# Low-key score products of a windowed attention layer in halves of TensorE's rows, on Trainium2

## The chip, the core and the metric
The kernel runs on one NeuronCore of a Trainium2 chip. The metric is the time on the device in microseconds for one execution of the whole program. The engines are TensorE (PE in the profile; its weight loads have a row of their own, PEld), VectorE (DVE), ScalarE (ACT), GpSimd (POOL) and SyncE (SP), which issues most DMAs.

## The reference, cut to what matters
Two groups of 512 tokens pass through the same two layers: layer A (latent attention) and layer B (windowed attention with 16 query heads, 2 key heads and 64 channels a head). The change lies in layer B, in this part:

```python
def swa_mixer(q, k, v, q_norm, k_norm, sink):
    q = rmsnorm(q.reshape(B, S, SWA_HEADS, SWA_HEAD_DIM), q_norm)
    k = rmsnorm(k.reshape(B, S, SWA_KV_HEADS, SWA_HEAD_DIM), k_norm)
    ...
    rel = jnp.arange(3 * BLOCK)[None, :] - BLOCK - jnp.arange(BLOCK)[:, None]
    in_window = jnp.abs(rel) <= WINDOW
    ...
        s = jnp.einsum('bqkgd,bjkd->bkgqj', q_blk, k_blk).astype(jnp.float32) * scale
        s = jnp.where(valid, s - slopes * dist, NEG)
        ...
        p = jax.nn.softmax(jnp.concatenate([s, sk], axis=-1), axis=-1)[..., :-1]
        return jnp.einsum('bkgqj,bjkd->bqkgd', p.astype(v_blk.dtype), v_blk)
```

With blocks of 128 tokens, query block i of the four meets the key blocks i-1 to i+1 that exist: 256 keys for blocks 0 and 3, 384 for blocks 1 and 2.

## The kernel before
The program runs four layers in turn, L = 0 to 3: A and B of the first group of tokens, A and B of the second. Every product keeps nearly full fp32 precision by splitting operands into a high part, rounded to fp32r, and a low part, the rest. A product of split operands is three matmuls: high by high, high by low, low by high (`mm3`).

In layer B the 64 channels of a head fill only half of TensorE's 128 rows, so the queries are stacked. `b_q(j)` handles head pair j: TensorE transposes the pair's queries into one bank (`b_q` of the TensorE part, line 2365), 64 rows for each head. ACT copies each half times its gain to `qT[half(a), j % 3, a, :]` as the high part (function `hi`, its activations have the line L859), and DVE writes the low part into the other half of the rows (function `lo`, L1283). `b_k(c)` puts the keys into `krT[:, 0, 0, :]` (high) and `krT[:, 0, 1, :]` (low), each twice, in both halves of the rows. One matmul over 128 rows then gives (high + low query) by high key, a second one by low key: `mm2`, lines 2063 and 2064. The low by low part, which the second one adds, is not needed.

`b_s(h)` makes the scores of head h: two matmuls for each of the four query blocks, in three banks: block 1, block 2, and blocks 0 and 3 together (`SHARED`, `SHARED_AT`). Each bank is told full after its last product. On DVE `b_max` (L1789) adds the bias and finds the maximum, and so frees the banks; ACT's `b_exp` (L886) and GpSimd's `b_p` (L1928) make the probabilities; `b_pt` (TensorE transposes L2102, ACT copies L859, DVE L1281, all to `probT`) turns them; `b_o` (L2415) multiplies them by the values; `b_low` (ACT, L1210, to `o_low`) and `b_sum` (DVE, L1803, to `o_pair`) add up high and low columns of the output.

The order on TensorE is written out by hand. Before the loop: projections, `b_q(0)`, `b_k(0)`, projections, `b_s(0)`, `b_q(1)`, ... In the loop over h = 0 to 15: `b_s(h + 2)`, projection steps (`fill`), `b_q(h // 2 + 2)` for even h up to 10, `b_o(h)`, projection steps, `b_pt(h + 1)`. ACT's and DVE's queues follow the same order: on ACT for an even h the copies of `b_q`, then `b_low(h)`, the tanh of gates that are complete (L896), the exps of head h + 2 and the copies of `b_pt(h + 1)`; on DVE `b_max(h + 2)`, the low halves of `b_q`, the gates (L1375), `b_sum(h)` and the low halves of `b_pt(h + 1)`.

Banks are handed on by counting semaphores: `vacant(use)` waits until the bank's use before has been read, `full(use)` tells that TensorE is through, `read(use)` that its reader is. A planner at the head of the file gives out banks; the scores of head 9 get for their first bank the one that `b_o(6)` wrote and `b_sum(6)` reads. `hi_done` counts ACT's high copies; a `lo` on DVE waits until as many are done as stood before it, plus `ahead`.

Of the kernel before, what the change touches and what calls it, by code (L numbers as in the profile page):

```python
# [11 lines left out]
P = 128  # L12
# [400 lines left out]
def span(i):  # L413

    return (window(i)[1] - window(i)[0] + 1) * P
# [6 lines left out]
def trunk_kernel(nc, kept, x, mem, mem_cols, w_a, w_b, w_out, w_mem, w_qb, w_kvb, gains, rope_gq, rope_gk, sink, cos, sin,  # L422
# [3 lines left out]
    with ctx:  # L426
# [4 lines left out]
        def place(name, shape, dt, at=None):  # L431

            size = int(np.prod(shape[1:])) * 4
            off = top[0] if at is None else at
            if at is None:
                top[0] += (size + 31) // 32 * 32
            return nc.alloc_sbuf_tensor_at(name, shape, dt, offset=off), off
# [25 lines left out]
        q_st, o_q = place("q_st", [P, NT, 2 * QK], fp32)  # L463
        k_st, o_k = place("k_st", [P, NT, 2 * QK], fp32)
        probT2, _ = place("probT2", [P, 2, 2 * 3 * P + CH], fp32r, o_q)
        c_st, _ = place("c_st", [P, NT, QR + KVR], fp32, o_q)
        k_mem_st, _ = place("k_mem_st", [P, NM, MW], fp32, o_k)
        sq, _ = place("sq", [P, 2, CH], fp32)
# [46 lines left out]
        with ExitStack() as turn, ExitStack() as block_end:  # L515
# [69 lines left out]
            def bank(use):  # L585
                return psum[USES[use][0]]
# [14 lines left out]
            def read(use):  # L601

                return bank_read[USES[use][0]], USES[use][1]
# [14 lines left out]
            def vacant(use):  # L618

                return bank_read[USES[use][0]], USES[use][1] - 1  # L620
# [56 lines left out]
            def half(a):  # L677

                return slice(64 * a, 64 * a + 64)
# [154 lines left out]
            def _(act):  # L834
# [20 lines left out]
                def hi(use, out, in_, gain=None, first=True):  # L855

                    if first:
                        act.wait_ge(*full(use))
                    act.activation(out, in_, ACT.Copy, scale=1.0 if gain is None else gain).then_inc(hi_done, 1)  # L859
# [126 lines left out]
                for L in range(LAYERS):  # L986
# [179 lines left out]
                    else:  # L1166
# [12 lines left out]

                        def b_q(j):  # L1180
                            for a in range(2):
                                hi(("bqT", L, j), qT[half(a), j % 3, a, :], bank(("bqT", L, j))[half(a), :],
                                   gcol[half(a), GAIN_AT["bq"]:GAIN_AT["bq"] + 1], first=a == 0)

                        def b_k(c):
                            hi(("bkT", L, c), krT[:, 0, 0, :], bank(("bkT", L, c))[:], gcol[:, GAIN_AT["bk"]:GAIN_AT["bk"] + 1])
# [66 lines left out]
            def _(dve):  # L1253
# [251 lines left out]
                for L in range(LAYERS):  # L1505
# [235 lines left out]
                    else:  # L1741
# [20 lines left out]
                        def b_q(j):  # L1762
                            for a in range(2):
                                lo(("bqT", L, j), qT[half(1 - a), j % 3, a, :], bank(("bqT", L, j))[half(a), :],
                                   qT[half(a), j % 3, a, :], gcol[half(a), GAIN_AT["bq"]:GAIN_AT["bq"] + 1], last=a == 1)

                        def b_k(c):
                            lo(("bkT", L, c), krT[:, 0, 1, :], bank(("bkT", L, c))[:], krT[:, 0, 0, :],
# [283 lines left out]
            def _(pe):  # L2052
# [8 lines left out]
                def mm2(out, lhs, rhs, start):  # L2061

                    nc.tensor.matmul(out, lhs, rhs[0], start=start, stop=False)  # L2063
                    return nc.tensor.matmul(out, lhs, rhs[1], start=False, stop=True)  # L2064
# [78 lines left out]
                for L in range(LAYERS):  # L2143
# [217 lines left out]
                    else:  # L2361
# [18 lines left out]
                        def b_s(h):  # L2380
                            pe.wait_ge(*read(("bqT", L, h // 2)))
                            pe.wait_ge(*read(("bkT", L, h // (HB // KVB))))
                            for s, blocks in enumerate(SHARED):
                                use = ("bS", L, h, s)
                                pe.wait_ge(*vacant(use))
                                for i in blocks:
                                    c = SHARED_AT[i][1]
                                    ins = mm2(bank(use)[:, c:c + span(i)], qT[:, (h // 2) % 3, h % 2, i * P:(i + 1) * P],
                                              tuple(krT[:, 0, a, window(i)[0] * P:(window(i)[1] + 1) * P] for a in range(2)), True)
                                ins.then_inc(full(use)[0], 1)  # L2390

                        def b_pt(h):
                            for s, blocks in enumerate(SHARED):
# [106 lines left out]
```

## Time and profile before

| | us |
|---|---|
| median of the runs | 1351.1 |
| lowest and highest of 3 runs | 1350.52, 1354.14 |
| the profiled execution | 1349.92 |
| its span in the profile | 1348.1 |

| engine | busy us | share of the span |
|---|---|---|
| PE | 1339.7 | 99% |
| PEld | 1163.8 | 86% |
| DVE | 890.7 | 66% |
| ACT | 678.0 | 50% |
| POOL | 395.3 | 29% |

The first layer B's attention lies at about 515 to 648 us, the second's at 1183 to 1315. Times in rows are counted from the span's start. Matmuls are pipelined: the duration of one reaches from its start to its modelled end, and the next one starts while it is still under way, so the pace of TensorE is read from starts. Consecutive equal instructions stand in one row of a timeline, with their count behind the x and the time from the first one's start to the last one's end. A bracket at the end of a row gives the engine's idle time before it and the instruction that ended it.

### The profile page before, as it was taken

Reading aid. Unit: us, or ns where it says so; the run is one execution under the profiler, and the core shown is the slowest. Engines: PE = TensorE matmul, PEld = TensorE weight load, DVE = VectorE, ACT = ScalarE, POOL = GpSimd, SP = SyncE. Lnnn points to the kernel's source line nnn. Section 1 sums busy time; section 2 is a strip of 40 time slices with the busy share of each in tenths; the row PEclk is TensorE's granted clock in tenths of the full one; section 3 lists DMA queues with packets and bytes.
Section 4 is the critical chain, followed back from the end, with each engine's and each line's share of the span. In section 5 each row is a group of like instructions: output and inputs, shape, how many; then the busy total and the mean of one; then the engine's idle time right before and its main releaser. Section 6 shows DMA issues by size and latency. Waiting matters only on the chain.

```text
span 1348.1 us, 20503 instructions
## 1 busy us (share of the span) xinstructions
PE 1339.7 (99%) x7160; PEld 1163.8 (86%) x7160; DVE 890.7 (66%) x1811; ACT 678.0 (50%) x1544; POOL 395.3 (29%) x511
## 2 busy tenths in 40 slices
PE   9999999999999999999999999999999999999999
PEld 7889888888888889988888898888888888899887
DVE  6776688878796757888582524767766634267871
ACT  6554466545565546777451413545444323157760
POOL 0421251330011323846202213423300122337560
PEclk9999999999999999999999999999999999999999
DMA  8958745334779797541875545333144652654325
GB/s 313 333 211 287 254 145 172 129 137 136 253 240 397 264 360 264 201 151 47 319 259 189 180 157 181 106 110 95 49 150 155 203 174 80 217 178 151 103 75 187
DMA packets 111926, 256.59 MB, mean 190 GB/s; under 512 B 11344, under 2 KB 49104, under 8 KB 111824
## 3 DMA queue, kind: packets, MB, share of 16 engines
q1 hardware_dynamic: 106352, 247.58, 53.0%
q10 hardware_dynamic: 5472, 7.69, 1.8%
q8 instruction: 59, 0.97, 0.3%
q14 instruction: 43, 0.35, 0.1%
HBM read 167.15 MB, written 88.08 MB: 189 GB/s over the span
## 4 chain that ended last, share of the span: by engine, by line
PE 89%; DVE 4%; ACT 2%; DMA 2%; issue 1%; POOL 1%; SPq 0%; ACTq 0%; DVEq 0%; POOLq 0%
PE bank L2057 25%; PE bank L2059 25%; PE bank L2058 25%; PE bank L2102 8%; PE bank L2415 3%; PE bank L2063 2%; PE bank L2064 2%; DMA w_raw<-in_w_mem 1%; DVE w_split L1269 1%; ACT prob L886 1%; DVE probT L1281 1%; DMA w_raw<-in_w_a 0%; DMA w_split<-kept_w 0%; DVE prob L1789 0%; ACT w_split L849 0%
## 5 line engine op out<-in xcount | busy, mean ns | idle before, releaser
L2057 PE MATMUL bank<-actT,w_split 128*128 128x512 f32 x544 | 214.9, 395 | 0.0
L2059 PE MATMUL bank<-actT,w_split 128*128 128x512 f32 x544 | 212.2, 390 | 0.0
L1928 POOL TENSOR_TENSOR prob<-prob,rinv 128x256 f32<-128x256 f32 x192 | 131.0, 714 | 247.8 <-DVE rinv L1443 247.8
L1269 DVE TENSOR_TENSOR w_split<-w_raw,w_split 128x512 fp32r<-128x512 f32 (+3 forms) x204 | 142.0, 708 | 81.6 <-ACT w_split L849 78.9
L849 ACT ACTIVATE w_split<-w_raw 128x512 fp32r<-128x512 f32 (+3 forms) x204 | 122.3, 607 | 126.6 <-DMA kept_w<-w_split 57.8
L2057 PE MATMUL bank<-w_split,actT 128*128 128x512 f32 (+3 forms) x512 | 171.2, 334 | 0.8 <-DMA w_split<-kept_w 0.4
L2058 PE MATMUL bank<-w_split,actT 128*128 128x512 f32 (+3 forms) x512 | 170.2, 332 | 0.0
L2059 PE MATMUL bank<-w_split,actT 128*128 128x512 f32 (+3 forms) x512 | 170.2, 332 | 0.0
L2058 PE MATMUL bank<-actT,w_split 128*128 128x512 f32 x384 | 149.9, 390 | 0.0
L1281 DVE TENSOR_TENSOR probT<-bank,probT 128x512 fp32r<-128x512 f32 (+1 forms) x192 | 112.1, 639 | 21.7 <-ACT probT L859 19.5
L868 ACT ACTIVATE sq<-bank 128x512 f32<-128x512 f32 (+4 forms) x128 | 60.4, 480 | 129.9 <-PE bank L2059 123.1
L859 ACT ACTIVATE probT<-bank 128x512 fp32r<-128x512 f32 (+1 forms) x192 | 94.0, 564 | 60.9 <-PE bank L2102 59.8
L1293 DVE TENSOR_REDUCE ss<-sq 128x2 f32<-128x384 f32 (+5 forms) x120 | 63.0, 541 | 90.9 <-ACT sq L868 90.1
L2059 PEld LDWEIGHTS bank<-actT,w_split 128*128 128x128 f32 x544 | 102.1, 188 | 21.9
L2057 PEld LDWEIGHTS bank<-actT,w_split 128*128 128x128 f32 x544 | 102.2, 188 | 19.0 <-DMA w_split<-kept_w 0.3
L886 ACT ACTIVATE prob<-bank,nmax 128x256 f32<-128x256 f32 (+1 forms) x128 | 72.9, 580 | 82.4 <-DVE nmax L1555 50.6
L2057 PEld LDWEIGHTS bank<-w_split,actT 128*128 128x128 f32 x512 | 96.9, 189 | 10.2 <-DVE w_split L1269 1.9
L1908 POOL TENSOR_TENSOR brlo<-gate,actT 128x512 fp32r<-128x512 f32 x40 | 52.1, 1307 | 178.6 <-ACT actT L906 178.6
L2059 PEld LDWEIGHTS bank<-w_split,actT 128*128 128x128 f32 x512 | 96.9, 189 | 7.6
L2058 PEld LDWEIGHTS bank<-w_split,actT 128*128 128x128 f32 x512 | 96.9, 189 | 7.5
L1866 POOL TENSOR_TENSOR rr<-rtmp,mhalf 128x4 f32<-128x4 f32 (+2 forms) x83 | 92.5, 1115 | 6.9
L2102 PEld LDWEIGHTS bank<-ident,prob 128*128 128x128 f32 x704 | 80.6, 140 | 9.3 <-DVE xs L1425 0.8
(197 smaller groups left out, 3065.3 us busy)
## 6 DMA issues: line engine op xcount, KB each, us to landing
w_split<-kept_w SPq DMA_DIRECT2D x120, 512.0 KB, 4.0
kept_w<-w_split SPq DMA_DIRECT2D x104, 512.0 KB, 5.6
w_raw<-in_w_mem SPq DMA_DIRECT2D x64, 256.0 KB, 3.4
kept_w<-part_split SPq DMA_DIRECT2D x32, 512.0 KB, 5.0
part_split<-kept_w SPq DMA_DIRECT2D x30, 512.0 KB, 4.1
w_raw<-in_w_b SPq DMA_DIRECT2D x44, 256.0 KB, 5.0
w_raw<-in_w_out SPq DMA_DIRECT2D x38, 256.0 KB, 4.5
w_raw<-in_w_a SPq DMA_DIRECT2D x32, 256.0 KB, 4.7
```

The lines of the kernel that those rows point to most:

```text
L849: act.activation(halves(n)[0], w_raw[:, r % RAW, 0:width], ACT.Copy).then_inc(w_hi_done, 1)
L859: act.activation(out, in_, ACT.Copy, scale=1.0 if gain is None else gain).then_inc(hi_done, 1)
L886: ins = act.activation(out, in_, ACT.Exp, bias=nmax[:, par, c:c + 1], scale=scale, accum_out=sums_of[:, par, c, 0:1])
L1269: dve.tensor_tensor(halves(n)[1], w_raw[:, RAW_AT[n] % RAW, 0:width], halves(n)[0].bitcast(fp32), ALU.subtract).then_inc(w_lo_dve, 1)
L1281: ins = dve.tensor_tensor(out, in_, hi_part, ALU.subtract)
L1293: dve.reduce_sum(out, v, AX).then_inc(sq_read, 1)
L1866: nc.gpsimd.tensor_tensor(dst, rtmp[:, 0:n], mhalf[:, 0:n], ALU.pow).then_inc(signal, 1)
L1928: pool.tensor_tensor(t, t, rinv[:, par, i:i + 1].to_broadcast(list(t.shape)), ALU.mult).then_inc(p_pool, 1)
L2057: nc.tensor.matmul(out, lhs[0], rhs[0], start=start, stop=False, skip_group_check=skip)
L2058: nc.tensor.matmul(out, lhs[0], rhs[1], start=False, stop=False, skip_group_check=skip)
L2059: return nc.tensor.matmul(out, lhs[1], rhs[0], start=False, stop=stop, skip_group_check=skip)
L2102: ins = nc.tensor.transpose(bank(use)[:, c * P:(c + 1) * P], src, ident[:])
```

## The change
The second product of each query block, by the low keys, takes 64 rows in place of 128, that is the high queries alone. For blocks 0 and 3 these are the rows `half(e)` of `qT`, where e says which head of the pair it is. For blocks 1 and 2 the same queries must stand in the other half of the rows: ACT copies them once more, from columns 128 to 384 of the bank, to a new tile `q_middle`, of two buffers. It lies behind `probT2` in memory that layer B doesn't use otherwise.

`b_s(h)` first makes the four products by high keys over 128 rows, for blocks 1, 2, 0, 3, and then two pairs of products over 64 rows by low keys: block 0 in one half of the rows with block 1 in the other, then block 3 with block 2. The two of a pair write different banks. The banks are told full with the last product that each gets, all three in the two pairs.

On ACT each `b_q(j)` has four copies in place of two, in the order high part, middle blocks, high part, middle blocks. On DVE the low halves count them: `lo` waits for one more copy than before.

```diff
+        q_middle, _ = place("q_middle", [P, 2, 2 * P], fp32r, o_q + 2 * (2 * 3 * P + CH) * 4)
...
                         def b_q(j):
                             for a in range(2):
-                                hi(("bqT", L, j), qT[half(a), j % 3, a, :], bank(("bqT", L, j))[half(a), :],
-                                   gcol[half(a), GAIN_AT["bq"]:GAIN_AT["bq"] + 1], first=a == 0)
+                                gain = gcol[half(a), GAIN_AT["bq"]:GAIN_AT["bq"] + 1]
+                                hi(("bqT", L, j), qT[half(a), j % 3, a, :], bank(("bqT", L, j))[half(a), :], gain, first=a == 0)
+                                hi(("bqT", L, j), q_middle[half(1 - a), j % 2, :], bank(("bqT", L, j))[half(a), P:3 * P], gain, first=False)
...
                                 lo(("bqT", L, j), qT[half(1 - a), j % 3, a, :], bank(("bqT", L, j))[half(a), :],
-                                   qT[half(a), j % 3, a, :], gcol[half(a), GAIN_AT["bq"]:GAIN_AT["bq"] + 1], last=a == 1)
+                                   qT[half(a), j % 3, a, :], gcol[half(a), GAIN_AT["bq"]:GAIN_AT["bq"] + 1], last=a == 1, ahead=1)
+                                count("hi")
...
+                            def scores(i, q, rows, a, start):
+                                s, c = SHARED_AT[i]
+                                keys = slice(window(i)[0] * P, (window(i)[1] + 1) * P)
+                                return nc.tensor.matmul(bank(("bS", L, h, s))[:, c:c + span(i)], q, krT[rows, 0, a, keys], start=start, stop=a == 1,
+                                                        skip_group_check=True)
+
+                            r, e = (h // 2) % 3, h % 2
                             for s, blocks in enumerate(SHARED):
-                                use = ("bS", L, h, s)
-                                pe.wait_ge(*vacant(use))
+                                pe.wait_ge(*vacant(("bS", L, h, s)))
                                 for i in blocks:
-                                    c = SHARED_AT[i][1]
-                                    ins = mm2(bank(use)[:, c:c + span(i)], qT[:, (h // 2) % 3, h % 2, i * P:(i + 1) * P],
-                                              tuple(krT[:, 0, a, window(i)[0] * P:(window(i)[1] + 1) * P] for a in range(2)), True)
-                                ins.then_inc(full(use)[0], 1)
+                                    scores(i, qT[:, r, e, i * P:(i + 1) * P], slice(0, P), 0, i == blocks[0])
+                            for i, other in ((0, 1), (3, 2)):
+                                outer = scores(i, qT[half(e), r, e, i * P:(i + 1) * P], half(e), 1, False)
+                                scores(other, q_middle[half(1 - e), (h // 2) % 2, (other - 1) * P:other * P], half(1 - e), 1, False).then_inc(
+                                    full(("bS", L, h, SHARED_AT[other][0]))[0], 1)
+                            outer.then_inc(full(("bS", L, h, 2))[0], 1)
```

## Rows read from the trace of the kernel before

**Rows 1.** The page's first part: busy us, share of the span, instructions.
```profile
PE 1339.7 (99%) x7160; PEld 1163.8 (86%) x7160; DVE 890.7 (66%) x1811; ACT 678.0 (50%) x1544; POOL 395.3 (29%) x511
```

**Rows 2.** Windows: stretch, us, busy of PE, PEld, DVE, ACT, POOL (x), clock, DMA share, GB/s.
```profile
515.00:648.00 133.00, 132.10 (x821) 118.94 (x821) 107.31 (x274) 97.90 (x256) 76.57 (x95) 1.00 0.43 147
```

**Rows 3.** Waits of PE over the span: us in total, times.
```profile
PE bank L2063 <- DVE o_pair L1803: 0.3, 2, 0.2
```

**Rows 4.** Timeline of PE, scores of head 3: start us, us, engine line op tiles xcount.
```profile
539.91 1.25 PE L2102 MATMUL bank<-ident,prob 128*128 128x128 f32 x10
540.92 0.42 PE L2063 MATMUL bank<-krT,qT 128*128 128x384 f32 x1
541.18 0.34 PE L2064 MATMUL bank<-krT,qT 128*128 128x384 f32 x1
541.35 0.35 PE L2063 MATMUL bank<-krT,qT 128*128 128x384 f32 x1
...
541.96 0.28 PE L2063 MATMUL bank<-krT,qT 128*128 128x256 f32 x1
...
542.19 0.39 PE L2057 MATMUL bank<-actT,w_split 128*128 128x512 f32 x1
```

**Rows 5.** Weight loads of the scores: ns min/median/max, first and last start, forms.
```profile
L2063 PEld LDWEIGHTS bank<-krT,qT x192: 186/188/192, 183.7 to 1298.1; 128*128 128x128 f32 x192
```

**Rows 6.** Groups by form, ACT, 515 to 648 us: xcount | busy us, mean ns | idle.
```profile
L886 ACT ACTIVATE prob<-prob,nmax 128x384 f32<-128x384 f32 x32 | 19.4, 606 | 1.9 <-DVE nmax L1789 1.7
L886 ACT ACTIVATE prob<-prob,nmax 128x256 f32<-128x256 f32 x32 | 15.8, 497 | 0.1
L859 ACT ACTIVATE qT<-bank,gcol 64x512 fp32r<-64x512 f32 x16 | 10.9, 683 | 12.3 <-PE bank L2102 12.1
```

**Rows 7.** Timelines of ACT, DVE and PE before the first scores.
```profile
518.69 0.69 ACT L859 ACTIVATE krT<-bank,gcol 128x512 fp32r<-128x512 f32 x1
519.53 0.75 DVE L1283 SCALAR_TENSOR_TENSOR krT<-bank,gcol,krT 128x512 fp32r<-128x512 f32 x1
520.39 0.41 PE L2063 MATMUL bank<-krT,qT 128*128 128x384 f32 x1
```

**Rows 8.** Timelines of ACT, DVE and PE, head 2 to `b_o(3)`.
```profile
551.80 1.39 ACT L859 ACTIVATE qT<-bank,gcol 64x512 fp32r<-64x512 f32 x2 [1.97 <-PE bank L2102]
557.86 1.62 DVE L1281 TENSOR_TENSOR probT<-bank,probT 128x384 fp32r<-128x384 f32 x3
559.14 1.34 PE L2415 MATMUL bank<-probT,v 128*128 128x384 f32 x8
```

**Rows 9.** Timelines of DVE and PE, the same place in the second layer B.
```profile
1225.75 1.62 DVE L1281 TENSOR_TENSOR probT<-bank,probT 128x384 fp32r<-128x384 f32 x3
1227.04 1.34 PE L2415 MATMUL bank<-probT,v 128*128 128x384 f32 x8
```

**Rows 10.** Timelines of DVE and PE, head 4 to `b_o(5)`.
```profile
571.07 1.62 DVE L1281 TENSOR_TENSOR probT<-bank,probT 128x384 fp32r<-128x384 f32 x3
572.36 1.42 PE L2415 MATMUL bank<-probT,v 128*128 128x384 f32 x8
```

**Rows 11.** Timelines of ACT, DVE and PE, head 6 to the scores of head 9.
```profile
581.33 1.09 ACT L896 ACTIVATE gate<-bank 128x512 f32<-128x512 f32 x2
580.85 1.52 DVE L1283 SCALAR_TENSOR_TENSOR qT<-bank,gcol,qT 64x512 fp32r<-64x512 f32 x2
583.60 0.68 DVE L1803 SCALAR_TENSOR_TENSOR o_pair<-bank,o_low 64x512 f32<-64x512 f32 x1
584.42 0.41 PE L2063 MATMUL bank<-krT,qT 128*128 128x384 f32 x1 [0.17 <-DVE o_pair L1803]
```

**Rows 12.** Timelines of DVE and PE, head 0 to `b_o(1)`.
```profile
541.77 1.62 DVE L1281 TENSOR_TENSOR probT<-bank,probT 128x384 fp32r<-128x384 f32 x3
543.58 1.34 PE L2415 MATMUL bank<-probT,v 128*128 128x384 f32 x8
```

**Rows 13.** Who waited for PE's L2064: us, times.
```profile
  DVE prob L1789: 0.4, 1
```

## Prediction

> **What bounds the kernel now.** I read the page first. TensorE is busy for 1339.7 of 1348.1 us [rows 1], but ends of matmuls are modelled, so that alone doesn't say that it is at its limit. The windows over the two layers B, the only stretches that the change touches, show the same there (132.1 of 133 us in the first), at a granted clock of 1.00, with ACT busy for 97.9 us, DVE for 107.3, DMA under half [rows 2]. The waits of TensorE are few: the one that concerns the scores is 0.3 us behind DVE's o_pair [rows 3]. So work taken off TensorE is worth its full length, unless a wait that is now just covered comes out.
>
> How full the engine is, one has to read from starts. In the timeline of one head [rows 4] the eight score products begin at 540.92 and the next projection at 542.19: 1.27 us for a head. The durations (0.28, 0.34) overlap. From start to start a 256-column product takes 0.12 us (two from 541.96 to 542.19), a 384-column one 0.17 (541.18 to 541.35), that is 107 and 160 ns of columns at 2.4 GHz and about 13 more. Ten transposes take 1.01 us, 0.10 to 0.11 each, though their 128 columns would stream in 0.053: there the weight loads set the pace, about 0.109 us each. The step between the two kinds costs next to nothing: the first score product after the transposes takes 0.26 instead of 0.17, but the ten transposes 1.01 instead of 10 x 0.109 = 1.09.
>
> **What the change does to TensorE.** Count per head: before, eight products over 128 rows, 2 x (384+384+256+256) = 2560 columns. After: four over 128 rows (high keys) and four over 64 rows (low keys with the high queries alone), as (256, 384), (256, 384). The number of matmuls and weight loads stays eight. What is gained depends on how two products in different halves of the rows run, which nothing in this trace shows: the score products' weight loads, all 192 of either line, have 128 rows as every other load in it [rows 5]. The four that change take 0.12+0.17+0.12+0.17 = 0.59 us now.
> Bounds. If each pair lasts as long as its longer member, they take 2 x 0.174 = 0.35 and 0.24 us a head are saved. If the members run one after the other, nothing is. Between: a second member can't start before its own weights are in. With loads 0.109 apart (the pace of the transposes) the four start at 0, 0.11, 0.22, 0.33, the last one's 384 columns end at 0.50, and 0.09 is saved. I take this, since the transposes are the only row that shows loads as the limit, and four loads in 0.59 us are what the pair is made of. Below nothing: going from 128 rows to halves and back could empty the engine. A 256-column product lasts 0.28 and starts the next after 0.12, so 0.16 us are in flight; twice a head that is up to 0.33 us lost. I take 0 for it, the value that the step to and from transposes shows, and keep the other end.
> The Trainium skill speaks against this choice: its page "TensorEngine Tiling (Array Packing)", section Key Properties, says that changing the tiling mode drains TensorE. No row here has two tiling modes. By it the sum would be that of rival 1.
>
> **What it does to ACT and DVE.** Each b_q(j) gets two more ACT copies of 64x256, in between the two of 64x512 that are there. Price: a qT copy is 0.683 us [rows 6]; 128 fewer columns are worth 0.606-0.497 = 0.109 in the exps, so 256 fewer 0.22: 0.465, with the 0.02 between two such copies (two take 1.39) 0.49. Two: 0.98 us for each of 16 b_q (8 in each layer B), in ACT's line ahead of whatever ACT has behind it. DVE gets no instruction, but each lo waits for one more copy. ACT has idle time, but these copies stand where it has none: they start on the transposes' end, and o_low, the gates' tanh, the exps and the copies of the next probabilities follow without a gap until TensorE needs their result. So I went through each place:
> - Before the first scores: qT, qT, krT on ACT, then krT's low half on DVE, which ends at 519.53+0.75 = 520.28; scores start at 520.39 [rows 7]. No cover. The two copies come ahead of krT, so it starts at 518.69+0.98 = 519.67 and ends at 520.36, and its low half runs from 520.4 to 521.2. TensorE waits about 0.85 us. The second layer B runs the same chain.
> - Head 2: the qT copies start at 551.80 and ACT has no gap from there to the probT copies. DVE's low halves end at 557.86+1.62 = 559.48. Head 3's b_o starts at 559.14 and needs the last of them after four 384-column products, at 559.84 [rows 8]. Cover 0.36, about 0.05 of it for the handover. 0.98 comes through: 0.65 us of waiting. In the second layer B the same distance is there: 1225.75+1.62 = 1227.37 against 1227.04+0.70 [rows 9].
> - Head 4: DVE ends at 571.07+1.62 = 572.69, b_o of head 5 starts at 572.36 and needs it at 573.08 [rows 10]: cover 0.39, wait 0.6, in both layers.
> - Head 6: the scores of head 9 wait for o_pair of head 6, which ends at 584.28; they start at 584.42, 0.17 us idle, a wait that is there today [rows 11]. DVE reaches its qT halves only at 580.85, 0.87 after the first copy's end, so these shift by 0.1 only and end at 582.45; but the two tanh start at 582.31 instead of 581.33, the first ends at 582.9, and the gate products start then instead of at 582.40: o_pair ends about 0.55 later. Wait 0.55, both layers. That covers head 7, whose distance (0.8) would otherwise be short too.
> - Head 0: low halves end at 543.39, needed at 543.58+0.70 = 544.28 [rows 12]: 0.15 of waiting; in the second layer B ACT has no weights to split there and it is covered. Heads 8 and 10 have 1.4 us of distance: nothing.
> Sum: 2 x (0.85+0.65+0.6+0.55) + 0.15 = 5.45 us lost.
> Against it the saving, 0.09 a head for 32 heads. But scores that lie between a b_q and the wait behind it only lengthen that wait: heads 3 (one layer), 5 and 7 of the score order, and the last one or two heads of a layer, which wait already: 7 in all. 25 x 0.088 = 2.2 us.
>
> **Edits at nothing.** The scores' banks are full later: the first after six products instead of two, about 0.5 us. Behind it is b_max on DVE, which in both layers B together waited for scores once, 0.4 us [rows 13]: DVE comes to it late from its own probT work, and that hides the delay. If that cover went, b_max, exp and GpSimd's product would have a further 2 to 3 us before the transposes two half-steps on. The other start flag and the smaller product (low times low left out) change no column. No DMA, queue or buffer moves.
>
> **Sum.** The profiled execution is 1349.9 us (span 1348.1 and 1.8 around it), the median of the runs 1351.1, 1.2 more. -2.2 + 5.45 = +3.25: 1353.2 for such an execution, 1354.4 for the median.
>
> **Rivals.**
> 1. The halves cost a switch. Each change from 128 rows to 64 and back lets what is in flight run out: 0.33 us a head. For: nothing shows that it is free. Against: transposes to products is free. It decides from 0.044 us a switch on, where it eats the pair's saving. At the full price 27 x (0.33-0.09) = 6.4, with ACT's 5.45: 1363. Slower, clearly.
> 2. The pair runs fully side by side, weight loads too: 25 x 0.24 = 6.0 against 5.45: 1350.5, and faster beyond the bound only if half of ACT's waits stay away as well (1348). The Trainium skill's page "TensorE: Matmul & The Clock Gate", section The mechanism, has the members of such a pack start about 4 ns apart; that would be this case. For: half as many rows to load. Against: a load of 128 columns sets the pace of the transposes.
> 3. The change doesn't do what it says: the members run one after the other. 0 against 5.45: 1356.6.
> 4. ACT's copies cost nothing (I misjudge the cover). Then 32 x 0.09 = 2.8 faster: 1348.3. Against: DVE and ACT rows stand in line, with 0.1 to 0.4 us of distance.
>
> **Chances.** Mine 0.38 (own range 1351.5 to 1357), rival 1 in some size 0.28, rival 2 0.14, rival 3 0.13, rival 4 0.07. 0.3% is 4.05 us, about what a measurement of this kernel tells from no change. Slower beyond it: rival 1 nearly all (0.26), most of rival 3 (0.1), a quarter of mine (0.1): 0.46. Faster beyond it: 0.1, from 2 and 4. Same: 0.44. Range: 1348.5 (rivals 2 and 4) to 1363 (rival 1 at full price).
>
> **What would show it.** In the changed profile: the starts of a head's eight score products. Mine: half-row starts 0.11 apart, head 1.18 us. Rival 1: a hole before the first half-row product and before the projection that follows. Rival 2: members under 0.02 apart. Rival 3: 0.12 and 0.17 as now. For ACT: 32 more copies of 0.47 us, 16 in each layer B, the first scores at about 521.2 in place of 520.4 (TensorE waiting for krT or probT of DVE), and waits before the b_o of heads 3 and 5 and before the scores of head 9. Wrong would be a saving per head over 0.15 or a loss, or TensorE waits that don't grow by 4 to 6 us.

## The result and the profile after

| | us |
|---|---|
| median of the runs, changed kernel | 1362.7 (1361.55 to 1364.63, 4 runs) |
| median of the runs, kernel before | 1350.81 (1350.02 to 1354.14, 4 runs) |
| ratio, 95% interval | 1.0087 (1.0074 to 1.0099) |
| the profiled execution, its span | 1363.76, 1362.0 |

The change makes the kernel slower by 11.9 us, or 0.9%. The granted clock is 1.00 as before. The page and the window over the first layer B answer to [rows 1, 2]:

```profile
PE 1349.2 (99%) x7160; PEld 1155.9 (85%) x7160; DVE 890.1 (65%) x1811; ACT 691.8 (51%) x1576; POOL 396.0 (29%) x511
```

```profile
515.00:648.00 133.00, 130.34 (x795) 110.30 (x794) 103.59 (x269) 102.34 (x267) 73.06 (x93) 1.00 0.42 143
```

In the same 133 us TensorE starts 795 products instead of 821. Outside the score products of the 32 heads, the list of 7160 products is the same in both kernels and stands in the same order, so one can lay the steps from start to start beside each other. From the first copy of queries to the last `o_low`, the first layer B is 5.72 us longer and the second 5.79: 11.5 us in the two profiled executions, while the medians are 11.9 apart. They fall into two parts.

**Part one, the head itself.** TensorE's timeline at one head's scores, then its weight loads at the same place (start us, us, engine, line, tiles, xcount; answers to [rows 4, 5]):

```profile
580.39 1.16 PE L2390 MATMUL bank<-krT,qT 128*128 128x384 f32 x5
581.16 0.44 PE L2390 MATMUL bank<-krT,q_middle 64*128 64x384 f32 x1
581.38 0.28 PE L2390 MATMUL bank<-krT,qT 64*128 64x256 f32 x1
581.44 0.34 PE L2390 MATMUL bank<-krT,q_middle 64*128 64x384 f32 x1
581.71 0.50 PE L2060 MATMUL bank<-actT,w_split 128*128 128x512 f32 x1
582.04 0.39 PE L2061 MATMUL bank<-actT,w_split 128*128 128x512 f32 x1
```

```profile
581.16 0.18 PEld L2390 LDWEIGHTS bank<-krT,q_middle 64*128 64x128 f32 x1
581.27 0.19 PEld L2390 LDWEIGHTS bank<-krT,qT 64*128 64x128 f32 x1
581.27 0.19 PEld L2390 LDWEIGHTS bank<-krT,q_middle 64*128 64x128 f32 x1
581.71 0.19 PEld L2060 LDWEIGHTS bank<-actT,w_split 128*128 128x128 f32 x1 [0.25 <-issue]
```

The first pair's member in `qT` is the fifth product of the first row. It and its partner start 3 ns apart (581.159 and 581.162, unrounded), and so do the weight loads of a pair: the halves do run side by side. From there on each half goes at its own pace, so the second pair's members start 0.22 and 0.28 us behind the first's, and 0.06 apart. But around the group there are holes. The four 128-row products before it take 581.16 - 580.39 = 0.77 us, where [rows 4] give 0.26+0.17+0.12+0.12 = 0.67: 0.09 (by the unrounded starts) lost before the first half-row product. From 581.16 to the second product of the projection it takes 0.88, where before it is 0.59 for the four products and 0.23 for the first one of the projection, 0.82. Together the head and what follows cost 0.15 us more (582.04 - 580.39 = 1.65, where before it is 1.27 + 0.23 = 1.50), although the pairs run side by side. The load at 581.71 tells why: in the kernel before, loads run one product ahead even from the scores into the projection, as the load of the projection's first product shows (the second row is its second product):

```profile
542.08 0.19 PEld L2057 LDWEIGHTS bank<-actT,w_split 128*128 128x128 f32 x1
...
542.42 0.40 PE L2058 MATMUL bank<-actT,w_split 128*128 128x512 f32 x1
```

There the projection's weights start at 542.08 for a product at 542.19. After the half-row group they start at 581.71, with the product itself, behind 0.25 us in which nothing was loaded, and the step to the projection's second product is 0.33 instead of 0.23. So a change of rows lets the products run out, and the next weights aren't loaded ahead. The way into the halves costs the same two things: 0.09 lost before the first half-row product, and a load that starts with the product, so that the first `q_middle` product lasts 0.44 where the second lasts 0.34, as the projection's first lasts 0.50 where it lasted 0.39.

**Part two, waits behind ACT's copies.** ACT's groups by form (xcount | busy us, mean ns | idle; answers to [rows 6]) and the waits of TensorE (us in total, times, longest; answers to [rows 3]):

```profile
L860 ACT ACTIVATE qT<-bank,gcol 64x512 fp32r<-64x512 f32 x16 | 11.0, 686 | 12.8 <-PE bank L2105 12.6
L860 ACT ACTIVATE q_middle<-bank,gcol 64x256 fp32r<-64x256 f32 x16 | 7.5, 470 | 0.4
```

```profile
PE bank L2390 <- issue: 1.6, 2, 0.8
PE bank L2390 <- DVE o_pair L1806: 1.2, 2, 0.6
PE bank L2060 <- DVE probT L1283: 1.1, 2, 0.5
```

The 1.6 us put down to "issue" are the first scores of the two layers B. ACT, DVE and TensorE there (answers to [rows 7]):

```profile
518.37 0.68 ACT L860 ACTIVATE qT<-bank,gcol 64x512 fp32r<-64x512 f32 x1 [2.63 <-PE bank L2105]
519.08 0.47 ACT L860 ACTIVATE q_middle<-bank,gcol 64x256 fp32r<-64x256 f32 x1
...
520.78 0.69 ACT L860 ACTIVATE krT<-bank,gcol 128x512 fp32r<-128x512 f32 x1
...
521.58 0.75 DVE L1285 SCALAR_TENSOR_TENSOR krT<-bank,gcol,krT 128x512 fp32r<-128x512 f32 x1
...
522.43 1.13 PE L2390 MATMUL bank<-krT,qT 128*128 128x384 f32 x5 [0.80 <-issue]
```

DVE's low half of the keys ends at 522.33 and the scores start 0.1 later, as they did at 520.39 behind 520.28. So it is that half they wait for, whatever the bracket says. By start-to-start steps they come 0.94 us later than before. The copies add 1.0 to ACT's chain.

One more kind of wait stands inside the scores, and these rows hide it under the products in flight. `b_s` now asks for its second bank with the second product, where it was the third, and for its third bank with the third product, where it was the fifth. At head 7 the third product needs the bank that DVE's `b_sum` frees:

```profile
573.08 1.40 PE L2390 MATMUL bank<-krT,qT 128*128 128x384 f32 x5
574.10 0.44 PE L2390 MATMUL bank<-krT,q_middle 64*128 64x384 f32 x1
...
572.93 0.68 DVE L1806 SCALAR_TENSOR_TENSOR o_pair<-bank,o_low 64x512 f32<-64x512 f32 x1
```

`o_pair` ends at 573.61, and that product starts at 573.66. From 573.08 to 574.10 the head takes 1.02 us, against 0.77 above. By steps, and beyond the 0.15 of the pairs, heads 5, 7 and 13 lose 0.10, 0.26 and 0.26 us in this way, in either layer B (at head 5 the bank is one that DVE's gates free). It takes both halves of the change: of these 0.62 us, the kernel with the copies alone loses 0.10 (head 13) and the one with the pairs alone 0.03 (head 7).

### The profile page after: what moved, and what is told of

It is laid out like the page before. It is cut to its first block, busy times and chain, and to the rows that moved or that the text cites. A ratio compares the mean times of both kernels' runs of the same rounds, so it can differ in the third digit from the quotient of the medians.

```text
span 1362.0 us, 20535 instructions
## 1 busy us (share of the span) xinstructions
PE 1349.2 (99%) x7160; PEld 1155.9 (85%) x7160; DVE 890.1 (65%) x1811; ACT 691.8 (51%) x1576; POOL 396.0 (29%) x511
## 4 chain that ended last, share of the span: by engine, by line
PE 88%; DVE 4%; ACT 3%; DMA 2%; issue 2%; POOL 1%; SPq 0%; ACTq 0%; DVEq 0%; POOLq 0%
PE bank L2060 25%; PE bank L2062 24%; PE bank L2061 24%; PE bank L2105 8%; PE bank L2427 3%; PE bank L2390 2%; DMA w_raw<-in_w_mem 1%; PE bank L2066 1%; PE bank L2067 1%; DVE w_split L1271 1%; ACT prob L887 1%; DVE probT L1283 1%; DMA w_raw<-in_w_a 1%; ACT w_split L850 0%; DVE xs L1848 0%
## 5 line engine op out<-in xcount | busy, mean ns | idle before, releaser
L2105 PEld LDWEIGHTS bank<-ident,prob 128*128 128x128 f32 x704 | 80.5, 140 | 9.2 <-DVE xs L1427 0.6
```

The lines of the kernel that those rows point to most:

```text
L2105: ins = nc.tensor.transpose(bank(use)[:, c * P:(c + 1) * P], src, ident[:])
```

## The experiments

All of them were timed against the kernel before. The last column is how much longer the two layers B are in the profiled execution, added. In four of them (pairs only, all in one half, four changes, one group) SyncE's wait at the end of a layer B, ahead of loads for the next layer, also goes by the bank that is told full last, which the diffs below leave out.

| run | median us | before | ratio, 95% interval | layers B, us |
|---|---|---|---|---|
| complete change | 1362.7 | 1350.81 | 1.0087 (1.0074 to 1.0099) | +11.5 |
| copies only | 1359.78 | 1351.38 | 1.0061 (1.0048 to 1.0073) | +7.6 |
| pairs only | 1355.62 | 1351.38 | 1.0031 (1.0019 to 1.0042) | +4.6 |
| all in one half | 1362.77 | 1351.38 | 1.0087 (1.0072 to 1.0103) | +11.3 |
| four changes of rows | 1367.98 | 1351.38 | 1.0123 (1.0109 to 1.0137) | +16.1 |
| late copies | 1357.63 | 1351.06 | 1.0044 (1.0030 to 1.0058) | +5.7 |
| one group for two heads | 1352.84 | 1351.06 | 1.0008 (0.9999 to 1.0017) | +1.2 |
| pairs first | 1354.95 | 1351.06 | 1.0029 (1.0018 to 1.0041) | +4.5 |

The expectations decided between theory and rival in each case but one group, and were off in size. The copies cost more than I expected, alone (8.4 us against 5.5 to 6.5) and late (6.6 against 4 to 5). Where the changes of rows count, the time was below the expectation (11.4 against 13 to 14 for one half, 16.6 against 18 to 19 for four changes), since I had priced a change at 0.21 us and it is 0.19.

**Copies only.** The edits of ACT and DVE, with TensorE's scores as before.

```diff
 (kernel before)
+                                gain = gcol[half(a), GAIN_AT["bq"]:GAIN_AT["bq"] + 1]
+                                hi(("bqT", L, j), q_middle[half(1 - a), j % 2, :], bank(("bqT", L, j))[half(a), P:3 * P], gain, first=False)
...
+                                   qT[half(a), j % 3, a, :], gcol[half(a), GAIN_AT["bq"]:GAIN_AT["bq"] + 1], last=a == 1, ahead=1)
+                                count("hi")
```

> The copies of the middle blocks alone: ACT makes q_middle as in the change and DVE counts it, but nothing reads it, and TensorE's instructions are those of before. Theory (the copies stand where ACT has no gap, TensorE comes to wait for their followers): 5.5 to 6.5 us longer than before, with TensorE waiting before the first scores (about 0.9 a layer), before the value products of heads 3 and 5, before the scores of head 9 and before the projection behind the scores of head 11 (about 0.6 each), and the score products' starts as before, 1.27 us a head. Rival (the copies are hidden, and all 11.9 us come from TensorE's half-row products): within 1 us of before.

A head's eight products keep their 1.27 us. The copies alone cost 8.4 us. The waits of TensorE in this kernel (us in total, times, longest):

```profile
PE bank L2066 <- issue: 1.6, 2, 0.8
PE bank L2060 <- DVE probT L1283: 1.3, 3, 0.5
PE bank L2066 <- DVE o_pair L1806: 1.2, 2, 0.6
PE bank L2105 <- DVE probT L1283: 0.9, 2, 0.5
```

They are those of the complete change and one more (L2105, the transposes of `ks_b` ahead of `b_o(5)`). The idle times in such rows come out smaller than the steps from start to start, since they are counted from the modelled ends of products in flight. By steps, in the first layer B: first scores 0.94, projection behind the scores of head 2 0.48, `b_o(1)` 0.11, around `b_o(3)` 0.30 before it and 0.23 in it, `ks_b` 0.60, scores of head 9 0.43, projection behind the scores of head 11 0.73, and 0.3 in smaller ones (0.10 of it in the scores of head 13): 4.1.

**Pairs only.** TensorE's edit without ACT's copies: the middle blocks read what stands in the other half of `qT`, the low part of the queries, so their scores lack high query by low key. It measures time alone, and so do the kernels with four changes, with one group and with the pairs first.

```diff
 (changed kernel, with ACT's and DVE's lines as before)
-                                scores(other, q_middle[half(1 - e), (h // 2) % 2, (other - 1) * P:other * P], half(1 - e), 1, False).then_inc(
+                                scores(other, qT[half(1 - e), r, e, other * P:(other + 1) * P], half(1 - e), 1, False).then_inc(
```

> The pairs alone, no copies on ACT: the middle blocks' half-row product takes what lies in the other half of the rows of qT (the low part of the queries), so these scores lack high query by low key. TensorE's instructions, banks and signals are those of the change. Theory (per head two changes of row use at 0.21 us each against 0.24 us saved by the pairs, 0.16 lost): 32 x 0.16 = 5.2 us longer than before, and with the copies alone it adds up to the whole change. Rival (the copies are hidden): about 11.9 us longer.

TensorE at one head, from the first half-row product on, and its next weight load:

```profile
577.93 0.61 PE L2387 MATMUL bank<-krT,qT 64*128 64x256 f32 x4
578.48 0.50 PE L2057 MATMUL bank<-actT,w_split 128*128 128x512 f32 x1
...
578.47 0.19 PEld L2057 LDWEIGHTS bank<-actT,w_split 128*128 128x128 f32 x1 [0.24 <-issue]
```

The four take 0.55 us up to the projection. Two pairs side by side would need 2 x 0.174 = 0.35. The pairs cost 4.2 us by themselves, with no copy on ACT, so TensorE's part is a loss of its own. 4.2 and 8.4 add up to 12.6 against the 11.9 of both, which the intervals of the medians don't tell apart; in layers B it is 12.2 against 11.5. By steps a TensorE that is later waits less for ACT (0.21 in place of 0.60 at `ks_b`, 0.17 in place of 0.48 behind the scores of head 2), and loses part of that again in the bank waits of heads 5, 7 and 13.

**All in one half.** The low-key products over 64 rows in the same half, one after the other. They compute what the change computes, without `q_middle`.

```diff
 (changed kernel, with ACT's and DVE's lines as before)
-                                scores(other, q_middle[half(1 - e), (h // 2) % 2, (other - 1) * P:other * P], half(1 - e), 1, False).then_inc(
+                                scores(other, qT[half(e), r, e, other * P:(other + 1) * P], half(e), 1, False).then_inc(
```

> The four low-key products over 64 rows all in the same half (the half that holds the head's high queries), no copies: the changes of row use stay, the pairs can't run side by side. Theory (two changes of row use at 0.21, four products at their full pace of 0.12 or 0.17): 0.42 us a head, 13 to 14 us longer than before, about 8 more than the pairs alone; starts inside the group 0.12 and 0.17 apart. Rival (a half-row product exposes its own weight load, a change of rows costs nothing): starts inside the group 0.22 and 0.28 apart, also in the pairs; 0.4 a head.

```profile
579.41 1.61 PE L2387 MATMUL bank<-krT,qT 128*128 128x384 f32 x8
580.95 0.49 PE L2057 MATMUL bank<-actT,w_split 128*128 128x512 f32 x1
```

From 579.41 to 580.95 the head takes 1.54 us, against 1.31 with pairs (577.17 to 578.48 in the kernel with pairs only) and 1.27 before. Two things follow. Pairing is worth 0.23 us a head, what two products side by side should save (0.12 for each pair). The products in one half start 0.12 and 0.17 apart, as 128-row ones do. And the same eight products with the same columns as before cost 0.27 more in the head, and 0.11 in the step behind it, through nothing but the two changes of rows: 0.38.

**Four changes of rows.** Each pair right behind the 128-row products of its own two blocks, so that a head goes to halves and back twice.

```diff
 (kernel with pairs only)
-                            for s, blocks in enumerate(SHARED):
-                                pe.wait_ge(*vacant(("bS", L, h, s)))
-                                for i in blocks:
-                                    scores(i, qT[:, r, e, i * P:(i + 1) * P], slice(0, P), 0, i == blocks[0])
                             for i, other in ((0, 1), (3, 2)):
+                                for b in (other, i):
+                                    if b != 3:
+                                        pe.wait_ge(*vacant(("bS", L, h, SHARED_AT[b][0])))
+                                    scores(b, qT[:, r, e, b * P:(b + 1) * P], slice(0, P), 0, b != 3)
```

> As the pairs alone, but each pair stands right behind the 128-row products of its own two blocks: 128 rows, pair, 128 rows, pair, so four changes of row use a head instead of two. Same products, same widths; middle blocks again with the other half of qT's rows. Theory (each change costs 0.21): 0.58 us a head longer than before, 18 to 19 us in all, 13 more than with both pairs behind. Rival (no cost of a change, the loss lies in the half-row products themselves): the same as the pairs alone, 5 us.

A head from its first product to the projection, and TensorE's weight loads in it:

```profile
581.65 1.76 PE L2387 MATMUL bank<-krT,qT 128*128 128x384 f32 x8
583.34 0.50 PE L2057 MATMUL bank<-actT,w_split 128*128 128x512 f32 x1
...
582.12 0.19 PEld L2387 LDWEIGHTS bank<-krT,qT 64*128 64x128 f32 x2 [0.19 <-issue]
582.49 0.30 PEld L2387 LDWEIGHTS bank<-krT,qT 128*128 128x128 f32 x2 [0.18 <-issue]
582.97 0.19 PEld L2387 LDWEIGHTS bank<-krT,qT 64*128 64x128 f32 x2 [0.19 <-issue]
583.34 0.19 PEld L2057 LDWEIGHTS bank<-actT,w_split 128*128 128x128 f32 x1 [0.18 <-issue]
```

The first two rows are from 581.65 to the projection, the others the loads between. Each of the four changes has its hole in the loads, in either direction, 0.18 to 0.19 us long. The head takes 1.69 instead of 1.31: 0.38 for two more changes, 0.19 each. In 32 heads that is 12.2 us, and the median is 12.4 above that of the pairs alone. The price goes by the number of changes.

**Late copies.** The complete change, but ACT makes `q_middle` from `qT` in SBUF, behind the copies of `b_pt`, with a semaphore of its own that TensorE waits for before the pairs. DVE doesn't count them.

```diff
 (changed kernel, with DVE's lines as before)
-                                hi(("bqT", L, j), q_middle[half(1 - a), j % 2, :], bank(("bqT", L, j))[half(a), P:3 * P], gain, first=False)
...
+                        def b_q_middle(j):
+                            act.wait_ge(*read(("bqT", L, j)))
+                            for a in range(2):
+                                ins = act.activation(q_middle[half(1 - a), j % 2, :], qT[half(a), j % 3, a, P:3 * P].bitcast(fp32), ACT.Copy)
+                            ins.then_inc(q_middle_done, 1)
...
                                 b_pt(h + 1)
+                            if h % 2 == 0 and h + 4 < HB:
+                                b_q_middle(h // 2 + 2)
...
+                            pe.wait_ge(q_middle_done, HB // 2 * G + h // 2 + 1)
                             for i, other in ((0, 1), (3, 2)):
```

> The whole change, complete, with the two copies moved: ACT makes q_middle from qT in the on-chip memory instead of from the bank, behind its copies of the next head's probabilities, where it has been idle for 1 to 2 us, and a semaphore of its own tells TensorE; the low halves on DVE no longer wait for it. The number of copies, the pairs and their order are those of the change. Theory (the copies cost 6 to 8 us only by their place, the pairs 4 to 5): about 4 to 5 us longer than before, as the pairs alone, 1355 to 1356, and 7 faster than the change. Rival (the copies cost by being there, in ACT's time or the memory's): as the change, 1362.

This does all the work of the change and is 5.1 us faster (1357.63), since the copies' waits are gone but for one of 0.8, behind the scores of head 2 in the first layer B, and about 0.1 in the scores of head 7 of each. TensorE there, and ACT and DVE where it begins:

```profile
536.80 0.33 PE L2399 MATMUL bank<-krT,q_middle 64*128 64x384 f32 x1
537.85 0.47 PE L2069 MATMUL bank<-actT,w_split 128*128 128x512 f32 x1 [0.72 <-DVE probT L1293]
...
529.56 0.84 ACT L1190 ACTIVATE q_middle<-qT 64x256 fp32r<-64x256 f32 x2 [0.26 <-DVE qT L1295]
530.42 0.63 ACT L851 ACTIVATE w_split<-w_raw 128x512 fp32r<-128x512 f32 x1
...
531.09 0.69 DVE L1281 TENSOR_TENSOR w_split<-w_raw,w_split 128x512 fp32r<-128x512 f32 x1 [1.56 <-ACT w_split L851]
```

ACT's `w_split` stands behind the copies of `b_q(1)`, DVE waits 1.56 us for it (0.80 at the same place in the kernel before), and everything behind it on DVE is later, `b_max(1)` and with it `probT` of head 0. Layers B are 5.7 us longer here, of which the pairs alone make 4.6. So ACT's copies cost mainly by their place and not by their length: at the other place two take 0.84 us, and most of it is hidden. The run changes two more things along with the place, the source (SBUF instead of the bank) and DVE's wait for the copies, and doesn't tell how much each of the three is worth.

**One group for two heads.** Even heads make no low-key products, and odd heads make their own twice: four pairs in one group, half as many changes of rows and the same number of products.

```diff
 (kernel with pairs only)
-                            for i, other in ((0, 1), (3, 2)):
+                            if e == 0:
+                                return
+                            for n, (i, other) in enumerate(((0, 1), (3, 2), (0, 1), (3, 2))):
...
```

> One group of four pairs for every two heads: even heads get only their four 128-row products, odd heads get their own four and then their low-key products twice, in four pairs, middle blocks with the other half of qT's rows, no copies. The scores of even heads lack the low key, those of odd heads have it doubled: it measures time alone. The number of products is that of the change, the changes of row use are half as many. Theory (a change costs 0.21, a pair saves 0.12): two heads cost 0.42 - 0.48 - about 0 = 0.06 less to 0.17 less than before, 1 to 3 us shorter than before in all. Rival (the loss is in the half-row products themselves): 4 to 5 us longer, as the pairs alone.

The group of an odd head, and the wait ahead of that head's scores:

```profile
585.42 1.72 PE L2387 MATMUL bank<-krT,qT 128*128 128x384 f32 x12 [0.76 <-DVE o_pair L1803]
...
586.18 0.97 PE L2387 MATMUL bank<-krT,qT 64*128 64x256 f32 x8
587.08 0.50 PE L2057 MATMUL bank<-kT,part_split 128*128 128x512 f32 x1
```

Eight half-row products take 0.90 us, where four took 0.55: two more pairs cost 0.35, which is 2 x 0.174. That is the pure price of a pair, and it leaves 0.20 in the group, 0.09 before it and 0.11 behind it for the two changes: 0.40. The run is 2.8 us better than the pairs alone and no faster than the kernel before. The best that it could give is small: eight low-key products before take 2 x 0.59 = 1.18, four pairs 4 x 0.174 = 0.70 and the changes 0.38 to 0.40, about 0.1 saved for two heads and 1.5 us in all. Two heads without a wait show that 0.1: they and the steps behind them take 2.89 us, against 2.99 before. Waits such as the one in the first row (0.76 in place of the 0.17 of [rows 11]) took more than that. My expectation of 1 to 3 us faster was a miss: it left these waits out. A version with the correct sums for two heads would hold the banks of both heads' scores at once, and it wasn't tried, as it could save 1.5 us at best.

**Pairs first.** The pairs ahead of the 128-row products, right behind the transposes.

```diff
 (kernel with pairs only: the two loops in the other order, all three banks waited for ahead)
+                            for i, other in ((0, 1), (3, 2)):
+                                scores(i, qT[half(e), r, e, i * P:(i + 1) * P], half(e), 1, i == 0)
+                                scores(other, qT[half(1 - e), r, e, other * P:(other + 1) * P], half(1 - e), 1, True)
                             for s, blocks in enumerate(SHARED):
                                 for i in blocks:
-                                    scores(i, qT[:, r, e, i * P:(i + 1) * P], slice(0, P), 0, i == blocks[0])
+                                    ins = scores(i, qT[:, r, e, i * P:(i + 1) * P], slice(0, P), 0, False)
```

> Both pairs ahead of the head's four 128-row products, no copies, middle blocks with the other half of qT's rows: the change from 128 rows to halves now follows the transposes, the one back leads to score products. Banks are full in the order 1, 2, 0 and 3 again. Theory (a change of row use costs the same whatever kind of 128-row work is beside it): 4 to 5 us longer than before, as the pairs alone. Rival (what is behind the group matters, its loads or its columns): another 2 us or more from that, either way; in the starts, a hole other than 0.10 after the transposes and 0.21 after the group.

TensorE's products and weight loads at one head:

```profile
578.02 1.40 PE L2387 MATMUL bank<-krT,qT 64*128 64x256 f32 x8
579.25 0.40 PE L2057 MATMUL bank<-actT,w_split 128*128 128x512 f32 x1
...
578.02 0.30 PEld L2387 LDWEIGHTS bank<-krT,qT 64*128 64x128 f32 x4 [0.17 <-issue]
578.57 0.47 PEld L2387 LDWEIGHTS bank<-krT,qT 128*128 128x128 f32 x3 [0.25 <-issue]
```

The holes have moved along: one now lies between the transposes and the first half-row product, the other between the pairs and the 128-row products, and the projection's first product has its usual length again (0.40). The cost is the same (+4.5 against +4.6 us in layers B). So the hole belongs to the change of rows, not to the step into the projection. A step from transposes to 128-row products is nearly free, one from transposes to 64-row products isn't.

## Why the prediction was right or wrong

The measured median is inside the range, 0.3 us below its upper end, and on the side that had 0.46 of the chances. The forecast itself, 1354.4, was 8.3 us too low, and its own theory is not what happened: by the signs that it gave itself (a loss per head, waits that don't grow by 4 to 6 us) it was wrong. The time lies inside because the range reached up to rival 1. In the two layers B the sum was -2.2 + 5.45 = +3.25. Measured: +4.8 in the heads (32 x 0.15) and the remaining +6.7 in waits, +11.5. So 7.0 of the 8.3 us are the heads, about 1.3 the waits.

**The step that failed: "I take 0 for it", the cost of going to halves and back.** I took it from the step between transposes and products. Those differ in columns and in what they do, but both use 128 rows, so the row did not show the thing that I priced; "pairs first" shows that the transposes don't help. Measured, two changes cost 0.38 to 0.40 us by three ways: the same products in one half (0.38), two changes more (0.38), and a group taken apart (0.09 before it, 0.20 in it beyond the longer members, 0.11 behind it). The other end that I kept, 0.33 from the 0.16 us in flight, was near in size and incomplete in kind: beside the products that run out, the next weights aren't loaded ahead.

The Trainium skill, page "TensorEngine Tiling (Array Packing)", section Key Properties, says that a change of tiling mode drains TensorE; here the trace agrees, at about 0.2 us for each change.

**The pairs' saving in a head: 0.09 predicted, 0.23 measured.** I let loads follow each other at 0.109 us, the pace of the transposes. The loads of the two halves start together (581.27 and 581.27), so rival 2 had the mechanism of the pair. The Trainium skill, page "TensorE: Matmul & The Clock Gate", section The mechanism, has members start about 4 ns apart; here the trace agrees for the first pair of a group, 3 ns apart. The second pair's members start 0.06 us apart, as the half with 256 columns comes free earlier.

**The rivals.** Rival 1 named the time (1363) and the sign of what it would show: "a hole before the first half-row product and before the projection that follows" stands there. But its sum, 27 x (0.33 - 0.09) = 6.4, was 1.6 above what the heads lost, with errors that partly offset each other: the changes cost 0.38 to 0.40 and not 0.33, the pairs of a head save 0.23 and not 0.09, and 0.15 over all 32 heads is 4.8. ACT's 5.45 was 1.3 too low on top, so that the total of 1363 was met by luck. Rivals 1 and 2 were both true at once, and I had set them up as if they excluded each other. Rival 3 fell by the 3 ns, rival 4 by "copies only".

**ACT's copies: 5.45 predicted, 7.6 by themselves, 6.7 in the complete change.** The price of a copy was right (0.465 worked out, 0.470 measured). Place by place, in us for the first layer B, by start-to-start steps, with the pairs' 0.15 a head taken off:

| place | predicted | copies only | complete change |
|---|---|---|---|
| first scores | 0.85 | 0.94 | 0.94 |
| `b_o(1)`, and the projection behind the scores of head 2 | 0.15 | 0.59 | 0.17 |
| around `b_o(3)` | 0.65 | 0.53 | about 0.4 |
| `ks_b` ahead of `b_o(5)` | 0.6 | 0.60 | 0.21 |
| scores of head 9 | 0.55 | 0.43 | 0.41 |
| projection behind the scores of head 11 | 0 | 0.73 | 0.59 |
| banks inside the scores of heads 5, 7 and 13 | 0 | 0.10 | 0.62 |

The places from cover worked out by rows were near, though the wait predicted for `b_o(5)` came a step earlier, at `ks_b`. Two were missed, 0.6 us each in either layer B: the last row, which the section on edits at nothing should have held, and the projection behind head 11. TensorE's and DVE's rows at the latter, in the complete change and then in the kernel before:

```profile
606.32 0.34 PE L2390 MATMUL bank<-krT,q_middle 64*128 64x384 f32 x1
607.19 0.47 PE L2060 MATMUL bank<-kT,w_split 128*128 128x512 f32 x1 [0.54 <-DVE probT L1283]
...
606.49 0.56 DVE L1283 TENSOR_TENSOR probT<-bank,probT 128x384 fp32r<-128x384 f32 x1
```

```profile
600.33 1.02 DVE L1281 TENSOR_TENSOR probT<-bank,probT 128x384 fp32r<-128x384 f32 x2
...
601.24 0.40 PE L2057 MATMUL bank<-kT,w_split 128*128 128x512 f32 x1
```

I wrote "Heads 8 and 10 have 1.4 us of distance: nothing", and meant the distance to `b_o`, which reads `probT`. The projection in between needs the bank out of which DVE makes that `probT`. That distance was a quarter as long: in the kernel before the first of the two ends about 600.33 + 0.56 = 600.89, 0.35 ahead of the projection at 601.24. With ACT's chain later it ends at 606.49 + 0.56 = 607.05, and the projection, due at about 606.6, waits for it. The same bank wait stands behind the scores of head 2.

**The edits at nothing** held for banks that are full later: nobody waits for the score products in the profile of after, where `b_max` waited once, 0.4 us, before [rows 13] (with the pairs alone it waits twice, 1.2 us). That the new order also asks for two of the three banks earlier isn't in the prediction, and it is what the waits of 0.62 us a layer B come from, together with the later `o_pair` and gates.

Left open: by its span the profiled execution is 13.9 us longer, 11.5 of it in the layers B. Of the rest 1.1 us stands ahead of the first layer B and 1.2 between the two, where the kernels are alike, and the medians leave only 0.4 us for it. In the nine profiles the first layer B starts anywhere from 517.2 to 519.7 us, so this looks like spread between executions; its cause wasn't followed.

## What to carry to other kernels

Halves of TensorE's rows are only worth it in long groups: with pairs of (256, 384) columns that save about 0.12 us each and two changes of rows at 0.40 a group, four pairs in a group barely pay by the sum (the run came out even), and two lose. Before pricing a step between two kinds of instruction by a row that shows a free one, check that the row differs in the very property that the change alters. And when an engine's chain moves later, look not only for the reader of its result but for whoever takes the bank that it frees; and when an order changes, for banks that are now asked for earlier.

## What the runs showed of the hardware

- The first two 64-row products of a group, in different halves and with different banks, start 3 ns apart, and so do their weight loads. After that each half goes at its own pace, 0.12 us for 256 columns and 0.17 for 384. In a run of them two pairs of 256 and 384 columns take 0.35 us, that is the longer members' 0.174 each.
- A change between 128 and 64 rows costs about 0.2 us, either way and also from transposes: products run out (0.09 us), and the weight load of the first product behind it starts only with the product, after 0.17 to 0.25 us without a load, which shows as 0.10 to 0.11 in the following step (0.33 in place of 0.23).
- 64-row products one after the other in the same half keep the 128-row pace: head 1.54 us, which is 1.27 and the cost of the changes. Fewer rows save nothing by themselves.
- A copy of 64x256 out of PSUM takes ACT 0.470 us, 0.22 less than one of 64x512 (0.686).
